# Windowed attention in a two-block layer kernel: who divides the softmax weights, and in which order ScalarE and VectorE take the work of a step

## What is computed

```
logits = einsum('bnqgrd,bnkgd->bngrqk', qb, kb) * (64 ** -0.5)
logits = where(valid, logits + bias, -inf)
m = maximum(max(logits, axis=-1), sink)
p = exp(logits - m)
p = p / (sum(p, axis=-1) + exp(sink - m))
out = einsum('bngrqk,bnkgd->bnqgrd', p, vb)
```

## Time and profile before

| | us |
|---|---|
| median of 3 runs | 1902.14 (1901.55 to 1902.55) |
| the profiled execution | 1904.01 |
| its span on the core | 1902.3 |
| PE busy / DVE / ACT / POOL | 1851.0 / 894.2 / 784.8 / 1363.5 |
| granted TensorE clock over the span | 0.996 |

### The profile page before, as it was taken

How to read it: one execution, slowest core, us unless ns; L and a number is a source line. 1 busy time by engine, 2 the same in 40 slices (tenths; PEclk the granted TensorE clock), 3 DMA queues, 4 the chain that set the end, 5 groups by cost and what they waited for, 6 DMA issues and landing times.

```text
span 1902.3 us, 26191 instructions
## 1 busy us (share of the span) xinstructions
PE 1851.0 (97%) x9597; PEld 1563.5 (82%) x9597; DVE 894.2 (47%) x1765; ACT 784.8 (41%) x1495; POOL 1363.5 (72%) x1211
## 2 busy tenths in 40 slices
PE   7999999999999989999999999999999999999999
PEld 6888888888877777888888888897679888888887
DVE  6677777762026655345502421727652445203410
ACT  4577777754038893242101210568644522101100
POOL 8766666798844458978988988663434669988985
PEclk9999999999999999999999999999999999999999
DMA  7322222223332222422333333222022222333332
GB/s 219 111 67 67 67 67 67 67 67 110 111 95 62 62 73 89 136 69 93 104 88 106 93 90 109 67 62 67 27 80 95 90 67 89 89 104 95 88 106 71
DMA packets 213613, 165.71 MB, mean 87 GB/s; under 512 B 14478, under 2 KB 209873, under 8 KB 213122
## 3 DMA queue, kind: packets, MB, share of 16 engines
q1 hardware_dynamic: 208134, 149.32, 26.8%
q10 hardware_dynamic: 5372, 14.98, 2.4%
HBM read 161.11 MB, written 7.37 MB: 89 GB/s over the span
## 4 chain that ended last, share of the span: by engine, by line
PE 79%; POOL 6%; ACT 4%; issue 4%; DVE 3%; PEld 3%; PEldq 0%; DMA 0%; ACTq 0%; POOLq 0%; DVEq 0%; SPq 0%
PE bank L401 54%; PE bank L483 9%; POOL w_lo L3226 4%; PEld bank L401 2%; PE bank L451 1%; POOL w_hi L3218 1%; PE bank L427 1%; PE bank L1247 1%; PE bank L1584 1%; PE bank L1193 1%; PE bank L1244 1%; PE bank L1791 1%; PE bank L1608 1%; PE bank L2976 1%; PE bank L1223 1%
## 5 line engine op out<-in xcount | busy, mean ns | idle before, releaser
L3226 POOL TENSOR_TENSOR w_lo<-w_raw,w_hi 128x512 fp32r<-128x512 f32 (+1 forms) x572 | 716.8, 1285 | 207.8 <-ACT w_hi L1431 198.4
L3218 POOL TENSOR_TENSOR w_hi<-w_raw,one 128x512 fp32r<-128x512 f32 (+1 forms) x428 | 441.0, 1061 | 241.1 <-PE bank L401 217.7
L401 PE MATMUL bank<-h_hi,w_hi 128*128 128x512 f32 x952 | 381.3, 401 | 1.1 <-POOL w_lo L3226 0.8
L401 PE MATMUL bank<-h_hi,w_lo 128*128 128x512 f32 x952 | 372.0, 391 | 0.0
L401 PE MATMUL bank<-h_lo,w_hi 128*128 128x512 f32 x952 | 371.0, 390 | 0.0
L401 PE MATMUL bank<-a_hi,w_hi 128*128 128x512 f32 x832 | 326.1, 392 | 1.8 <-POOL w_lo L3226 1.4
L401 PE MATMUL bank<-a_hi,w_lo 128*128 128x512 f32 x832 | 324.0, 389 | 0.0
L401 PE MATMUL bank<-a_lo,w_hi 128*128 128x512 f32 x832 | 323.8, 389 | 0.0
L401 PEld LDWEIGHTS bank<-h_hi,w_lo 128*128 128x128 f32 x952 | 178.6, 188 | 38.9
L401 PEld LDWEIGHTS bank<-h_hi,w_hi 128*128 128x128 f32 x952 | 178.9, 188 | 36.1 <-issue 1.4
L401 PEld LDWEIGHTS bank<-h_lo,w_hi 128*128 128x128 f32 x952 | 179.2, 188 | 33.9
(11 more groups left out here) (502 smaller groups left out, 3033.9 us busy)
## 6 DMA issues: line engine op xcount, KB each, us to landing
w_raw<-in_w_ff SPq DMA_DIRECT2D x32, 1024.0 KB, 5.5
w_raw<-in_w_in SPq DMA_DIRECT2D x31, 1024.0 KB, 5.4
w_raw<-in_w_mlp_in SPq DMA_DIRECT2D x16, 1024.0 KB, 5.4
w_raw<-in_w_mlp_out SPq DMA_DIRECT2D x16, 1024.0 KB, 5.7
w_raw<-in_w_in SPq DMA_DIRECT2D x26, 512.0 KB, 4.4
w_raw<-in_w_ssd_out SPq DMA_DIRECT2D x8, 1024.0 KB, 5.7
bias_rows<-bias_row ACTq DMA_DIRECT2D x1, 4096.0 KB, 15.8
w_raw<-in_w_attn_out SPq DMA_DIRECT2D x4, 1024.0 KB, 6.0
```

What stands on the lines that cost most here:

```text
L401: mm = pe.matmul(bank[:, 0:ntok], a, b[:, koff + k, 0:ntok], start=(k == 0 and n == 0), stop=(k == L.kb - 1 and n == 2))
L3218: pool.tensor_tensor(w_hi[:, slot, part], raw[:, slot, part], one[:].broadcast_to([P, n]), ALU.mult).then_inc(split_hi, 1)
L3226: ins = pool.tensor_tensor(w_lo[:, slot, part], raw[:, slot, part], w_hi[:, slot, part].bitcast(F32), ALU.subtract)
```

## The change

The division of the weights is shared: VectorE multiplies those of even units by the reciprocal, in place, right after it (a `dve_link` is a wait of VectorE for its own last instruction); ScalarE does it for odd units only, in even steps. `high` on ScalarE and `low` on VectorE go to the front of a step, `below` and `out_high` to its end; on VectorE `summed` and `out_low` follow the reciprocal. Two semaphores of the split of queries, keys and values are merged into one with the counts adapted, and `wa_norm` becomes a pair.

```diff
-                pe.wait_ge(wa_norm, u + 1)
+                pe.wait_ge(wa_norm[u % 2], u // 2 + 1)
...
-                act.wait_ge(wa_inverse, u + 1)
-                act.activation(L, L, ACT.Copy, scale=stat[:, s + 3:s + 4]).then_inc(wa_norm, 1)
+                act.wait_ge(wa_inverse, (u + 1) // 2)
+                act.activation(L, L, ACT.Copy, scale=stat[:, s + 3:s + 4]).then_inc(wa_norm[1], 1)
...
+                if 3 <= u < ALL_UNITS + 3:
+                    high(u - 3)
+                if u < ALL_UNITS:
+                    probs(u)
+                if u % 2 == 0 and 2 <= u < ALL_UNITS + 1:
+                    normed_weights(u - 1)
                 if u > WEIGH_AT and u % REP == 1:
                     below((u - WEIGH_AT) // REP)
                 if u > WEIGH_AT and u % REP == 2:
                     out_high((u - WEIGH_AT) // REP)
-                if 3 <= u < ALL_UNITS + 3:
-                    high(u - 3)
-                if u < ALL_UNITS:
-                    probs(u)
-                if 1 <= u < ALL_UNITS + 1:
-                    normed_weights(u - 1)
...
-                dve.reciprocal(stat[:, s + 3:s + 4], stat[:, s + 1:s + 2]).then_inc(wa_inverse, 1)
+                if u % 2:
+                    dve.reciprocal(stat[:, s + 3:s + 4], stat[:, s + 1:s + 2]).then_inc(wa_inverse, 1)
+                    return
+                _, _, _, k0, k1 = window_unit(u)
+                L = LOGITS[u % 4][:, 0:(k1 - k0) * P]
+                dve_link(dve.reciprocal(stat[:, s + 3:s + 4], stat[:, s + 1:s + 2]))
+                dve.tensor_scalar(L, L, stat[:, s + 3:s + 4], None, ALU.mult).then_inc(wa_norm[0], 1)
...
                     logits(u)
+                if 3 <= u < ALL_UNITS + 3:
+                    low(u - 3)
                 if 1 <= u < ALL_UNITS + 1:
                     inverse(u - 1)
                 if u > WEIGH_AT and u % REP == 1:
                     summed((u - WEIGH_AT) // REP)
                 if u > WEIGH_AT and u % REP == 2:
                     out_low((u - WEIGH_AT) // REP)
-                if 3 <= u < ALL_UNITS + 3:
-                    low(u - 3)
```

More of the change, by code:

```diff
@@ L1724, in build_program @@
         ATTN_GATE = [xT[:, b, :] for b in range(DB)]
-        wq_hi, wkv_hi, wv_made = sem("wq_hi"), sem("wkv_hi"), sem("wv_made")
-        wa_norm, wa_lo, wa_copied, wa_out, wa_inverse = (sem(f"wa_{k}") for k in ("norm", "lo", "copied", "out", "inverse"))
+        wqkv_hi, wv_made = sem("wqkv_hi"), sem("wv_made")
+        wa_norm = [sem(f"wa_norm{k}") for k in range(2)]
+        wa_lo, wa_copied, wa_out, wa_inverse = (sem(f"wa_{k}") for k in ("lo", "copied", "out", "inverse"))
         UNITS = REP * T
@@ L1817, in window_q_act @@
             for i, rows in enumerate(HALVES):
-                act.activation(QS[g % 2][rows, 2 * b + i, :], acc(L, b)[rows], ACT.Copy).then_inc(wq_hi, 1)
+                act.activation(QS[g % 2][rows, 2 * b + i, :], acc(L, b)[rows], ACT.Copy).then_inc(wqkv_hi, 1)
         def window_q_dve(dve, g, b):
             L = L_attn[g][0]
-            dve.wait_ge(wq_hi, 4 * g + 2 * b + 2)
+            dve.wait_ge(wqkv_hi, 6 * g + 2 * b + 2)
             dve.wait_ge(acc_free, L.b0 + b)
@@ L1836, in window_kv_act @@
                 ins = act.activation(KS[g % 2][rows, 0, :], acc(L, 0, 0, 64), ACT.Copy)
-            ins.then_inc(wkv_hi, 1)
+            ins.then_inc(wqkv_hi, 1)
         def window_k_dve(dve, g):
             L = L_attn[g][1]
-            dve.wait_ge(wkv_hi, 2 * g + 1)
+            dve.wait_ge(wqkv_hi, 6 * g + 5)
             dve.wait_ge(acc_free, L.b0)
@@ L1850, in window_v_act @@
             act.wait_ge(acc_ready, L.b0 + 2)
-            act.activation(VSTACK[g % 2][:, :, 0:64], acc(L, 1)[:, 0:256].rearrange("p (t f) -> p t f", t=T), ACT.Copy).then_inc(wkv_hi, 1)
+            act.activation(VSTACK[g % 2][:, :, 0:64], acc(L, 1)[:, 0:256].rearrange("p (t f) -> p t f", t=T), ACT.Copy).then_inc(wqkv_hi, 1)
         def window_v_dve(dve, g):
             L = L_attn[g][1]
-            dve.wait_ge(wkv_hi, 2 * g + 2)
+            dve.wait_ge(wqkv_hi, 6 * g + 6)
             dve.wait_ge(acc_free, L.b0 + 1)
```

## The result

The changed kernel takes 1909.43 us in the median of 8 runs (1908.19 to 1914.3), the kernel before 1903.21 in 8 (1901.55 to 1905.81). The ratio is 1.0035, with a 95% interval of 1.0024 to 1.0047: slower by 6 to 7 us. A second set of runs on another occasion gave 1909.72 against 1902.40 us, ratio 1.0041 (1.0027 to 1.0055). The forecast had the sign and the mechanism, and less than half of the size: +2.9.

The account below looks back on a forecast made before the run. The prediction took TensorE, busy 97% of the span, as the bound. A chain sum of +2.6 us and +0.3 for GpSimd gave +2.9, a median of 1905.0 us; range 1899.5 to 1909.5.

Parts of the forecast that it names:

- TensorE's waits before turns as the ceiling: Attention stage: TensorE's 15.9 us idle before its 160 transposes (`turn`) is the most a gain can reach.
- ScalarE's relief not enough: Half of 64 divisions leave ScalarE, some 17 us of its time; only TensorE's idle time can come back.
- The chain: Steps 4m+1 to 4m+3: late `below`, `summed`, `out_high`, `out_low` hold back the next `logits`; round of units 19 to 23 +0.77 us.
- The layout: Instruction-by-instruction replay of four-step rounds under the new order; rounding up to 0.15 us a round, 2 us over 13.
- The chain's sum: Round changes add to +3.3 us at the `logits` of 63; two terms off at the stage's end leave +2.6.
- GpSimd beside VectorE: Multiplications and `out_low` lengthened beside GpSimd, each by 0 to 0.9 us; +0.3 us gets through, bounds 0 and +6.
- GpSimd in the way: Rival: one held-up multiplication or `out_low` per round in the chain, 0.5 us over 13 rounds; 1910 us, chance 0.17.
- The sharing of the division: VectorE takes 32 multiplications, 0.35 or 0.42 us each plus 0.2 for wait and link; alone they cost nothing.
- Signs in the profile: ScalarE some 17 us less busy, VectorE 11 to 14 more; TensorE idle before `turn` 17 to 21 us, units 4m and 4m+1.

Follow-up runs that it names:

- e5: Changed kernel with `below` and `out_high` on ScalarE moved right behind `high`, ahead of the exponential: 1889.93 us, stage -12.80 us against the kernel before.
- e8: Changed kernel with VectorE's `out_low` moved from the end of step 4m+2 to the end of step 4m+3: 1896.84 us, ratio 0.9969 to the kernel before.
- e3: Changed kernel with GpSimd's weight splits within the attention cut to 8 columns a piece, for timing only: 1909.69 us, stage 172.94 us; run again, 1906.84 us.

## Why the prediction was right and wrong

- **TensorE's waits before turns as the ceiling, ScalarE's relief not enough.** Right. The 15.9 us were there to be had: e5 gets 12.8.
- **The chain.** Right in each link, and shown by cutting it: e5 and e8. The layout gave 10.25 us for the round of units 19 to 23; it took 10.43, and 10.37 with the thin splits of e3. For the other kinds it gave 10.27, 10.70 and 11.04; in e3 they took 10.33, 10.84 and 11.12. The logits of unit 11 came 24.20 us after the first of all, against 23.78 before: +0.42, where the layout had +0.40. That match is luck: in e3 it is 23.94, so the chain gave +0.16 there and GpSimd 0.26.
- **The chain's sum** was +2.6; without the splits within the attention it is +4.1. From unit 11 on the layout was 0.05 to 0.15 us short in each round, as its own margin said, and 0.8 in the last one (11.64 where 10.83 was laid out). There the splits of `w_attn_out`, which e3 does not cut, lie beside `out_low`, which takes 1.11 us in place of 0.42. So about 0.8 of the missing 1.5 us is the layout's own error, and 0.7 is GpSimd again. VectorE in e3, then GpSimd:

```profile
723.81 1.11 DVE L1993 TENSOR_TENSOR a_lo<-arena,a_hi 128x256 fp32r<-128x256 f32 x1 [0.88 <-ACT a_hi L1934]
```

```profile
722.60 4.21 POOL L3226 TENSOR_TENSOR w_hi<-w_raw,one 128x512 fp32r<-128x512 f32 x4 [10.04 <-PE bank L401]
```

- **GpSimd beside VectorE: the step that failed.** It was put at +0.3 us, "since in most rounds `out_low` lands near the end of one of GpSimd's short pieces", with bounds of 0 and +6. It is 2.5 us, and 0.7 more in that last round: 3.2 of the 6.58, and the larger of the two terms that were too small. The forecast had seen that `out_low` now lies in the chain with no cover. It then guessed by where the instructions would land to a few tenths, when the layout itself was uncertain by that much. Its own figures allowed a better estimate: GpSimd works 40% of the time, and an `out_low` that meets it is 0 to 0.9 us longer, 0.45 in the middle, which is 0.18 us a round and 2.3 over 13 rounds. In the changed kernel 10 of the first 14 `out_low`s were longer than 0.44 us, by 0.05 to 0.7.
- **The range** (1899.5 to 1909.5) held 1909.43 at its very edge. The rival "GpSimd in the way" named 1910 and 0.5 us for each of 13 rounds; it was half right: the hold-up was some 0.2 us a round, the rest was the chain. That the time came out near the 1910 of this rival is in good part luck.
- **The sharing of the division.** "Alone it costs nothing" held nearly: 1.28 us in the old order. The layout did not say how much it saves in the new one; that was 15.8 us of an order that would have lost 22.4.
- **Signs in the profile.** VectorE's 14.2 us more, TensorE's 18.7 us before turns, the turns of units 4m and 4m+1, and the waits before `summed` and `out_low` came as written. ScalarE's busy time fell by 13.7, not 17, since its instructions overlap their neighbours by up to 0.1 us.

One reading would have misled: TensorE's idle time before turns rose only by 2.8 us (15.9 to 18.7), while the stage grew by 6.6. A turn that is not held starts 0.35 us after the scores of 384 keys; a held one is counted as idle only from the scores' end, 0.51 us after their start, so 0.16 us of each stall count as busy. With a slightly later start of the products behind it that is about 0.2 us for each of 18 stalls more (33 in place of 15), 3.6 us.

## What to carry to other kernels

This is drawn from one kernel. When two in-order engines pass work to each other, count the links between them in one period, not the busy time of either: an instruction that another engine waits for belongs where its own engine would wait anyway, here behind `high` and ahead of the exponential. "Least urgent last" was wrong here for instructions that have a waiting partner with work queued behind it. And when a replay by rows leaves an instruction uncovered in the chain, take for it the share of time in which it is disturbed times the mean disturbance, not its best case.

## What the runs showed of the hardware

`out_low` reads two operands in SBUF, and a multiplication by a column reads one and writes one; both were stretched beside GpSimd's splits (`out_low` from 0.41 us to as much as 1.48, in e5; the multiplication from 0.35 or 0.42 to as much as 1.46, in e8). With the thin splits of e3 both went back, to 0.42 or 0.43 and to 0.35 or 0.42, but for two `out_low`s (1.11 and 0.54) and one multiplication (1.14) beside the splits of `w_attn_out`. `low` and `summed`, which read a PSUM bank, stayed as they were (`summed` 0.83 to 0.85 us for its two in all of these kernels). The Trainium skill, page "SBUF — State Buffer", section "SBUF: two separate sides", has this as an exclusive lock on a shared port pair; the runs agree. The price of it within the attention of the changed kernel is 2.5 us by the stage (175.41 less 172.89 or 172.94).

The other surprise: TensorE's granted clock fell outside of the attention, in part at places that differ between executions. In e3 (columns as in the earlier trace rows, the third number from the end is the granted clock):

```profile
850.00:855.00 5.00, 4.37 (x27) 3.53 (x26) 1.24 (x1) 2.06 (x4) 5.00 (x5) 0.93 0.01 3
855.00:860.00 5.00, 5.00 (x18) 4.23 (x17) 0.34 (x2) 0.00 (x0) 1.05 (x1) 0.50 0.50 163
860.00:865.00 5.00, 5.00 (x25) 4.30 (x24) 2.45 (x4) 1.12 (x2) 1.04 (x1) 0.89 0.14 47
```

0.50 is the lower level of 1.2 GHz; 0.07, 0.50 and 0.11 of 5 us are 3.4 us of full clock lost, more than the 2.5 us that e3 had won in the attention. The changed kernel had 1.00 in the same stretch; the kernel before had 0.66 in 825 to 830. TensorE was busy throughout 845 to 850 in e3 and 4.37 us of the 5 in which the clock fell, there in part with three groups of eight products of one column (L646, at 851.29, 852.99 and 854.84). The same three groups ran at 1.00 in the changed kernel (853.28 to 857.41). Around 1450 us the clock fell in every trace of this case. What makes it fall in one execution and not in another is open. It is why the stage, and not the whole time, is the measure above.
